# First stage of a two-block forward pass: latent products started chunk by chunk, norm applied afterwards

## The reference, cut to what matters

```python
h = rms_norm(x, norm_mix_g[l])
proj = h @ w_in[l]
mla_cols, rw_cols, gate_cols = _split(proj, [MLA_COLS, RWKV_COLS, GATE_COLS])   # 416, 1984, 2048
...
c_q, c_kv, k_rope = _split(cols, [Q_LORA, KV_LORA, QK_ROPE])                     # 256, 128, 32
c_q = rms_norm(c_q, q_a_norm_g)
c_kv = rms_norm(c_kv, kv_a_norm_g)
q = (c_q @ w_uq).reshape(B, S, MLA_HEADS, QK_NOPE + QK_ROPE)
kv = (c_kv @ w_ukv).reshape(B, S, MLA_HEADS, QK_NOPE + V_HEAD)
...
k_rope = rope(rms_norm(k_rope, kr_g), cos, sin)
```

## Time and profile before

| | us |
|---|---|
| median of 3 runs | 3447.28 (3444.87 to 3449.14) |
| the profiled execution's own time | 3440.47 |
| its span in the trace | 3438.7 |
| TensorE busy | 3199.9 (93%) |
| VectorE busy | 2036.8 (59%) |
| ScalarE busy | 1073.5 (31%) |
| GpSimd busy | 315.1 (9%) |
| mean granted TensorE clock | 0.963 |

### The profile page before, as it was taken

The page is one execution under the profiler, slowest core; times in us unless marked ns, Lnnn a source line. Parts: engine busy times, 40 slices in busy tenths (PEclk is TensorE's granted clock), DMA queues, the critical chain, the costliest instruction groups (busy, mean ns, idle before and its releaser), DMA issues.

```text
span 3438.7 us, 52047 instructions
## 1 busy us (share of the span) xinstructions
PE 3199.9 (93%) x22004; PEld 2553.4 (74%) x22004; DVE 2036.8 (59%) x3230; ACT 1073.5 (31%) x1526; POOL 315.1 (9%) x306
## 2 busy tenths in 40 slices
PE   7898999688888887999999999999998999999999
PEld 6686787566666666877888888877755888778887
DVE  3655454367677667534454454447979887645445
ACT  3222334344444443213111111122234333423332
POOL 0123342000000001310000000000000000000000
PEclk9999999799899988999999999999999999999999
DMA  3242665334333333430111111111101223223222
GB/s 140 76 142 79 204 222 195 64 78 103 84 98 80 82 79 121 145 126 28 60 49 49 49 49 48 43 45 37 37 25 49 81 93 109 74 74 123 98 98 74
DMA packets 93527, 301.86 MB, mean 88 GB/s; under 512 B 10352, under 2 KB 38640, under 8 KB 70768
## 3 DMA queue, kind: packets, MB, share of 16 engines
q1 hardware_dynamic: 79104, 246.63, 23.0%
q0 software_dynamic: 14192, 51.91, 4.4%
HBM read 241.35 MB, written 57.15 MB: 87 GB/s over the span
## 4 chain that ended last, share of the span: by engine, by line
PE 75%; DVE 11%; issue 4%; ACT 4%; DMA 3%; POOL 2%; SPq 1%; DVEq 0%; ACTq 0%; POOLq 0%
PE ps L2370 24%; PE ps L308 20%; PE ps L466 6%; PE ps L1724 3%; PE ps L2195 2%; PE ps L2512 2%; DMA Dn<-nbs 2%; PE ps L1713 2%; PE ps L1316 2%; PE ps L2030 1%; PE ps L437 1%; DVE Yh L2539 1%; PE ps L974 1%; PE ps L2390 1%; SPq L1667 1%
## 5 line engine op out<-in xcount | busy, mean ns | idle before, releaser
L2370 PE MATMUL ps<-Hh,whi 128*128 128x512 f32 x1600 | 498.1, 392 | 0.0
L284 ACT ACTIVATE whi<-raw 128x2048 fp32r<-128x2048 f32 x139 | 265.6, 1911 | 626.5 <-PE ps L308 310.5
L288 DVE TENSOR_TENSOR wlo<-raw,whi 128x2048 fp32r<-128x2048 f32 x139 | 318.8, 2294 | 172.5 <-ACT whi L284 171.9
L2370 PEld LDWEIGHTS ps<-Hh,whi 128*128 128x128 f32 x1600 | 300.3, 188 | 68.0 <-issue 6.2
L2370 PE MATMUL ps<-Hh,wlo 128*128 128x512 f32 x800 | 311.3, 389 | 0.0
L2370 PE MATMUL ps<-aHh,whi 128*128 128x512 f32 x512 | 199.8, 390 | 3.6 <-DVE xT L2716 2.5
L308 PE MATMUL ps<-Hlo,whi 128*128 128x512 f32 x656 | 202.0, 389 | 0.0
L308 PE MATMUL ps<-Hhi,wlo 128*128 128x512 f32 x656 | 201.9, 389 | 0.0
L308 PE MATMUL ps<-Hhi,whi 128*128 128x512 f32 x656 | 201.9, 389 | 0.0
L2370 PE MATMUL ps<-aLh,whi 128*128 128x512 f32 x512 | 199.2, 389 | 0.0
L2370 PE MATMUL ps<-aHh,wlo 128*128 128x512 f32 x512 | 199.2, 389 | 0.0
(11 more groups left out here) (378 smaller groups left out, 6244.4 us busy)
## 6 DMA issues: line engine op xcount, KB each, us to landing
raw<-in_panels SPq DMA_DIRECT2D x139, 1024.0 KB, 4.8
rwf<-F POOLq DMA_DIRECT2D x16, 1280.0 KB, 6.5
L<-rwf SPq DMA_DIRECT2D x16, 1024.0 KB, 5.0
L<-rwf SPq DMA_DIRECT2D x64, 256.0 KB, 4.2
Dn<-nbs SPq DMA_DIRECT2D x128, 128.0 KB, 5.0
gts<-so POOLq DMA_DIRECT2D x16, 512.0 KB, 3.2
gl<-gts SPq DMA_DIRECT2D x32, 256.0 KB, 3.3
rwt<-so POOLq DMA_DIRECT2D x15, 512.0 KB, 3.0
```

Of the source, the lines that this page charges most:

```text
L284: e.activation(whi[i % 2][:, :], raw_of(i)[:, :], AF.Copy).then_inc(*a_hi.up(i))
L288: e.tensor_tensor(wlo[i % 2][:, :], raw_of(i)[:, :], whi[i % 2][:, :].bitcast(F32), OP.subtract).then_inc(*v_lo.up(i))
L2370: m = e.matmul(ap, W[wi][:, kc, n0:n0 + 128], mov[mi][:, kc, :], start=x == 0 and q == 0, stop=x == len(kcs) - 1 and q == 2)
```

## The change

- The first chunk of x is followed by panel 0 in the queue of transfers; the constants come after chunk 3. 
- ScalarE makes all hi parts first, with panel 0 after chunk 0; the squares come later, two before panel 1 and six after the columns of mla0.
- VectorE makes the rest of panel 0 after chunk 0's, and makes the angles while it would wait for the sums.
- TensorE begins with mla0's products. The sums of squares follow them, then mla1's products.
- Columns are copied without the factor. The latents' sums of squares take it as a scale operand (`scale=rst`), and the three factors of a tile are multiplied by it (one small operation for a group). Squares stand in between the column copies, and norms are made in two groups, tiles 0 to 5 and 6 to 7.
- Panel 3's fetch is issued ahead of ukv and uq; uq also waits for the last square of x. The rest of panel 3 is made after the latents' norms.

The core of the diff:

```diff
@@ start_sp
         for kc in range(8):
-            if kc == 2:
+            if kc == 1:
+                panel_sp(e, 0)
+            if kc == 4:
                 e.dma_start(cc[:, :], A["consts"]).then_inc(*d_cc.up())
-            if kc == 3:
-                panel_sp(e, 0)
@@ new
+    def start_act(e):
+        e.wait_ge(*d_vec.by())
+        for kc in range(8):
+            e.wait_ge(*d_x.by(kc))
+            e.activation(Hhi[:, kc, :], xT[:, kc, :], AF.Copy, scale=vec("norm_mix_g", kc)).then_inc(*a_h.up(0, "hi", kc))
+            if kc == 0:
+                panel_act(e, 0)
+        squares_act(e, range(2))
+        panel_act(e, 1)
...
+    def lo_dve(e):
+        e.wait_ge(*d_vec.by())
+        for kc in range(8):
+            e.wait_ge(*a_h.by(0, "hi", kc))
+            e.scalar_tensor_tensor(out=Hlo[:, kc, :], in0=xT[:, kc, :], scalar=vec("norm_mix_g", kc),
+                                   in1=Hhi[:, kc, :].bitcast(F32), op0=OP.mult, op1=OP.subtract).then_inc(*v_h.up(0, "lo", kc))
+            if kc == 0:
+                panel_dve(e, 0)
+        panel_dve(e, 1)
@@ mla_pe, mla_act
             last_use[p] = (t_mla, (i, 7))
+            if i == 0:
+                rms_pe(e, 0, tmp)
...
-            e.activation(mlac[:, j, 208 * i:208 * (i + 1)], ring.bank("mla", i, j)[:, 0:208], AF.Copy,
-                         scale=rst[:, j:j + 1]).then_inc(*a_mla.up("cols", i, j))
+        e.activation(mlac[:, j, 208 * i:208 * (i + 1)], ring.bank("mla", i, j)[:, 0:208],
+                     AF.Copy).then_inc(*a_mla.up("cols", i, j))
@@ lat_act, lat_dve
+            m = e.activation(sq[:, o + 416 * (j % 2):o + 416 * (j % 2) + w], mlac[:, j, o:o + w], AF.Square,
+                             scale=rst[:, j:j + 1], accum_out=ss[:, j, n:n + 1])
...
+    LATJ = ((0, 6), (6, 8))
...
+        e.wait_ge(*g_lat.by("pow", g))
+        e.tensor_tensor(rsd[:, a_:z, :], rsd[:, a_:z, :], rst[:, a_:z, None].broadcast_to([128, z - a_, 3]), OP.mult).then_inc(*v_lat.up("scale", g))
@@ vector
+        lo_dve(e)
         start_dve(e)
-        rms_dve(e, 0, "norm_mix_g", rs)
+        angles_dve(e)
+        mean_of_dve(e)
         rst_dve(e)
-        panel_dve(e, 0)
-        panel_dve(e, 1)
-        for i in range(2):
-            panels_after(panel_dve, e, UIX[f"mla{i}"])
+        panels_after(panel_dve, e, UIX["mla0"])
         u_dve(e)
-        angles_dve(e)
+        lat_dve(e, 0)
+        lat_dve(e, 1)
+        panels_after(panel_dve, e, UIX["mla1"])
         front_dve(e)
@@ scalar
+        start_act(e)
+        for j in range(8):
+            mla_act(e, 0, j)
+        squares_act(e, range(2, 8))
+        sqrt_act(e)
+        panels_after(panel_act, e, UIX["mla0"])
         u_act(e)
         angles_act(e)
+        for j in range(8):
+            mla_act(e, 1, j)
+            if j >= 5:
+                for i in range(6) if j == 5 else (j,):
+                    lat_act(e, i)
+        panels_after(panel_act, e, UIX["mla1"])
         front_act(e)
```

More of the change, by code:

```diff
@@ L392, in start_sp, with squares_act, sqrt_act, mean_of_dve @@
         for kc in range(8):
-            if kc == 2:
+            if kc == 1:
+                panel_sp(e, 0)
+            if kc == 4:
                 e.dma_start(cc[:, :], A["consts"]).then_inc(*d_cc.up())
-            if kc == 3:
-                panel_sp(e, 0)
             e.dma_start(xT[:, kc, :], A["xT"][:, kc, :]).then_inc(*d_x.up(kc))
         panel_sp(e, 1)
+    def start_act(e):
[7 more added lines that the diff above has]
+        panel_act(e, 1)
+    def squares_act(e, kcs):
+        for kc in kcs:
+            if kc >= 2:
+                e.wait_ge(*t_h.by(0, "sum", kc - 2))
+            e.activation(tmp[kc % 2], xT[:, kc, :], AF.Square).then_inc(*a_h.up(0, "sq", kc))
+    def sqrt_act(e):
+        e.wait_ge(*v_h.by(0, "mean", 1))
+        e.activation(rs, rs, AF.Sqrt).then_inc(*a_h.up(0, "sqrt"))
+    def lo_dve(e):
[7 more added lines that the diff above has]
+        panel_dve(e, 1)
+    def mean_of_dve(e):
+        e.wait_ge(*t_h.by(0, "sum", 7))
+        for h in range(2):
+            e.tensor_scalar(rs[:, hs(h)], ring.bank("sum", 0, h), 1.0 / KB, 1e-6, OP.mult,
+                            OP.add).then_inc(*v_h.up(0, "mean", h))
+        e.wait_ge(*a_h.by(0, "sqrt"))
+        e.reciprocal(rs, rs).then_inc(*v_h.up(0, "rs"))
     def start_dve(e):
@@ L441, in mla_pe, with mla_act @@
             last_use[p] = (t_mla, (i, 7))
[L443 to L447, removed]
-            e.activation(mlac[:, j, 208 * i:208 * (i + 1)], ring.bank("mla", i, j)[:, 0:208], AF.Copy,
-                         scale=rst[:, j:j + 1]).then_inc(*a_mla.up("cols", i, j))
+            if i == 0:
+                rms_pe(e, 0, tmp)
+    def mla_act(e, i, j):
+        e.wait_ge(*t_mla.by(i, j))
+        e.activation(mlac[:, j, 208 * i:208 * (i + 1)], ring.bank("mla", i, j)[:, 0:208],
+                     AF.Copy).then_inc(*a_mla.up("cols", i, j))
     fring = banks(bank[4:6] + bank[2:4])
@@ L1116, in front_dve @@
                 rw_dve(e, i) if i < 16 else gt_dve(e, i - 16)
-            elif name == "lat":
-                lat_dve(e)
             elif name == "krope":
```

48 lines of the change are left out of this document (20 added, 28 removed).

## The result

The changed kernel took 3413.81 us (median of 4 runs, 3413.23 to 3417.45), the kernel before beside it 3446.07 (4 runs): a ratio of 0.9909 [0.9892, 0.9927]. The forecast was faster, at 3422 with a range from 3416. The direction and the mechanism hold; the number lies 8 us lower and outside the range. The profiled execution took 3413.23 us, its span is 3411.4, against 3438.7 before.

What follows compares the result with a forecast made beforehand. TensorE, busy 93% of the span, was the bound, so only its idle places could be won: 14.1 (start), 6.9 and 1.6 (waits), 2.8 (slow clock), together 25.4 us. 3447.3 - 25.4 gave about 3422 us, range 3416 to 3430.

Steps and rivals of the forecast that it cites:

- TensorE's start, and panel 0 at 8.3: Start of the kernel: panel 0 lands at about 8.3 us, TensorE's first latent product comes at 12.5 us.
- The first stretch, 35.6 to 49.3 to 70.7: TensorE's latents: mla0 ends at 35.6 us, sums of squares at 49.3, mla1 at 70.7 against 84.8 before.
- The way to channel 0: VectorE's list through the latents' squares and norms: channel 0 starts at 87.0 us against 112.39, 25.4 us earlier.
- the 1.03 under it: Latents' squares before channel 0: 1.03 us a tile from the kernel before, plus 0.09 for each of three scaled activations.
- What is late next: First head product: comes at 107.8 us after TensorE waits 3.3 us for `ckv` in place of 4.87; bank wait gone.
- I go by the row of 3.43, and take the loss to be the same as before: Behind the 3.3 us wait at the first head product: slow clock costs the same 1.5 us as before.
- The first costs nothing: TensorE's clock after a 2.43 us wait: it goes on at full pace, so nothing is lost beyond the wait.
- The failed step: Whole kernel: median stays 6.8 us above the profiled execution, 3447.3 - 25.4, with 2 to 3 us for the runs' spread.
- The scale is free: Latents' squares: scale from memory costs nothing, squares end 1.7 us earlier, 28.6 us won, 3419 us; chance 0.12.
- Panel 0 late: Start: panel 0 completes with chunks 1 to 3, 3.9 us later, 21.5 us won, 3426 us; chance 0.12.
- The old length of the chain: Latents' chain keeps its length as a group waits; only TensorE's start counts, 14.1 us won, 3433 us; chance 0.06.
- The clock not granted: TensorE stays at 1.2 GHz through mla0 and the sums, 30.2 us lost, slower at 3452 us; chance 0.03.

Runs made afterwards that it cites:

- panel0_late: Changed kernel with panel 0 queued behind chunks 1 to 3 and the constants; 3425.86 us, ratio 0.9938 to the kernel before.
- sums_rounded: Changed kernel with x's sums of squares made from rounded squares in one pass, seven tiles for squares; 3408.64 us, ratio 0.989 to the kernel before.
- latents_only: Kernel before with only the new places of angles, splits and latents' norms, in two groups, old start kept; 3427.68 us, ratio 0.9947.
- start_only: Kernel before with only the new start; angles, splits and latents' norms in old places, one group; 3430.36 us, ratio 0.9955.
- tuned: Changed kernel with panel 3's split moved into VectorE's pause and the second group's means inside the first group's norms; 3412.1 us, ratio 0.9904.
- both: Changed kernel with the edits of tuned and sums_rounded together; 3403.29 us, ratio 0.9881 to the kernel before.
- after_again: Changed kernel repeated with no edit; 3419.49 us (6 runs), ratio 0.992 to the kernel before; its profiled execution took 3421.63 us.
- after: First profiled execution of the changed kernel, no further edit; 3413.23 us.
- before_sixth: Kernel before repeated with no edit for one more profile; that execution took 3452.73 us.

## Why the prediction was right or wrong, by its steps

**TensorE's start, and panel 0 at 8.3: right.** It landed at 8.54, the first product came at 12.83 for 12.5, and panel0_late shows the dependence, 6.5 us for 6.5.

**The first stretch, 35.6 to 49.3 to 70.7: right.** 36.0, 49.4 and 71.2. The sums are on the path (sums_rounded), and the factor, the angles and the splits are hidden: VectorE waited 7.05 us before the first means.

**The way to channel 0: right to 0.5 us, one term over-sized.** Forecast 87.0, measured 86.47. The squares with the scale cost 1.18 us a tile, where I put 1.31. The price of the scale was right: each activation is 0.10 us longer (0.50 against 0.40 for 256 columns). What was over-sized is the 1.03 under it. In the kernel before the squares of a tile wait for those of the tile before (`a_lat.by("ss", j - 1)`), in the changed kernel for those of two tiles before, and the sum has no term for this. latents_only has the new wait and no scale; its tiles stand 0.90 us apart, 0.13 less than in the kernel before (87.29 to 88.32) and 0.28, three times 0.09, less than with the scale:

```profile
81.38 0.41 ACT L670 ACTIVATE sq<-mlac 128x256 f32<-128x256 f32 x1
...
82.28 0.40 ACT L670 ACTIVATE sq<-mlac 128x256 f32<-128x256 f32 x1
```

The 0.13 us are 0.8 over six tiles, and TensorE's start, 0.3 us later than forecast, takes part of it back.

**What is late next: right in kind, off in size.** No bank wait, and a wait for `ckv` of 2.27 us in place of 3.3: TensorE came at 105.0, half a microsecond behind the 104.5 of the sum, and VectorE half a microsecond ahead of its own. "I go by the row of 3.43, and take the loss to be the same as before" came true in the first trace after, with the same shape (a start at full pace, then half), and from there to the end it was 3304.1 us, against 3305.6 before, inside the 3 us that I gave. In three of the other four traces after it did not come true: no slow stretch, 1.6 us more kept. And "The first costs nothing", of the wait of 2.43 us, was the luck of two traces: it cost a slow stretch in four of six.

**The failed step** is the last one, from the profiled execution to the median: "The median of the runs is 6.8 us above that execution, and the same difference taken from it gives 3447.3 - 25.4", with "2 to 3 us for the runs' own spread". Against the profiled execution the sum gave 3415.1 and 3413.23 was measured. But the median of the result is only 0.6 us above its profiled execution, not 6.8, so the offset was no constant that goes over to the changed kernel. Single executions have a standard deviation of 4.3 us before (57 of them, mean 3446.6) and 2.9 after (18, mean 3417.1), and the one predicted from lies 6.1 us under the mean of its kernel. The gain over all is 29.5 us, uncertain by 1.8.

The traces account for it in this way: 25.9 up to the head product, 2.3 from there to the scan, 0.4 behind, which is nothing that can be told from chance. Where the offset itself comes from they show in part: against the one predicted from, the four later traces of before are 0.9 to 2.2 us longer up to the head product, 1.4 to 3.7 from there to the scan, and up to 7.4 from the scan on.

So of the 8.1 us between forecast and result 0.5 are for the head product, 0.7 for a median of three that lay above the mean of 57, and 3.6 for the gain beyond the head product (2.3 of it seen in the traces). The other 3.3 are there because the four runs of the result lie low among the changed kernel's own 18 (3413.2 to 3423.1); whether by chance or with the set is open, as the means of the three larger sets are 3414.6, 3419.1 and 3416.8. The mean of the 18, 3417.1, is inside the range, and the allowance of 2 to 3 us for the spread was less than these 3.3.

**The rivals.** The scale is free: out, it cost the 0.28 us a tile that were put for it (1.18 against the 0.90 of latents_only). Panel 0 late: out by the traces, where it landed at 8.54 to 9.65; panel0_late shows what a late one costs. The old length of the chain: out, though start_only is that case by construction (12.7 us to the head product; 14.1 had been worked out for it). The clock not granted, with the Trainium skill's warning behind it (TensorE: Matmul & The Clock Gate, "HAM oscillation — how this bites in real kernels"): out. The products went from 0.41 to 0.27 us in length at 16.4 and stayed there through the sums. In the other traces with the early start 15 to 31 of mla0's 192 products ran at half pace, which is at most 1.5 us more than in the first.

**What stays open.** The slow stretch behind the wait for `ckv` goes with the length of this wait: there after 4.6 us and more in all traces, after 2.3 in some, and gone where tuned and both have no wait. What decides after 2.3 us is open. Three of the six traces of before (130.4 to 131.2 us) are longer from the first L765 to the first L974 than any of after (128.7 to 129.5), and the stretch from there to the scan is 1.0 us longer on average. Why isn't shown; nothing in the change touches either, and with six and five traces it may be chance. The last 0.9 us of the 29.5 has no place in the traces at all, which is within their uncertainty.

## What to carry to other kernels

If a product can start before its norm is known, start it with the first chunk and multiply the factor in later; put the weight it needs second in the queue, since here every microsecond of its landing went through to the first head product. But follow both engines: the start alone kept only 12.7 of the 14 us, because the engine that has to follow (VectorE here) ran late on the same chain, and the second half of the gain came from making its list shorter at the same time. And a difference of some 0.1% has to come from many executions of both kernels, not from the offset of one profiled execution from a median of three.

## What the runs showed of the hardware

- One program's executions of 3447 us lie up to 16.7 us apart (3438.11 to 3454.77). In eleven traces of the two kernels the scan took 775.9 to 785.4 us with the same products, and VectorE, ScalarE and GpSimd each had the same busy time in it to 0.6 us. TensorE's was 8.5 us longer in after_again than in after, but only 0.9 in before_sixth (785.4 us) than in the first trace of before (778.5), so its pace is not all of it.
- In the seventeen traces (eight kernels) mla0 began at half pace and kept it for 15 to 31 of its 192 products, without a wait of TensorE in between. That is up to 1.5 us between two executions, before any other difference.
- A slow stretch behind a wait cost about 1.6 us (6 to 9 products at half pace in the eleven traces), and the same wait (2.43 us for `XN`) brings it in one execution and not in the next. So the price of a wait of 2 to 3 us is its length, or its length and 1.6.
- The granted clock that a profile gives can miss the first stretch: for 12.80 to 16.00 of the changed kernel it says 1.00, though the products are 0.41 us long, as long as such products are at half pace, and 0.27 only from 16.5. The kernel before has the same: 1.00 for 9.40 to 13.40, where the passes of the sums start 0.85 us apart, against 0.43 afterwards. The lengths of the products have to be read beside it.
- A scale from memory costs ScalarE 0.09 us for each short Square with an accumulator, and all of it is on the engine's path (a tile of three in 1.18 us with it, 0.90 without, in latents_only). A wait of ScalarE for its own last instruction cost 0.13 us a tile (1.03 against 0.90).
- GpSimd's power costs by the number: 1.33 us for 6 of each partition, 3.23 for 18, 4.17 for 24, about 0.16 each on 0.4. By these figures to split a norm into two groups costs one more 0.4, an estimate.
- VectorE's reciprocal of 128x1024 took 6.55 us, 6.4 ns for each of the 1024 elements of a partition, five times what an operation with two operands took on as many (1.28). It was hidden behind mla1 here.
